# Queries and keys of the first block: their halves exchanged by DMA inside SBUF instead of by a product with a permutation matrix

## The reference, cut to what matters

```python
proj = h @ w_in[l]
q, k, v, iq, ik, iw, z, xbc, dt_raw, ga, gm = jnp.split(proj, SPLIT_POINTS, axis=-1)
q = apply_rope(rms_norm(q.reshape(bsz, seq, 16, 64), q_norm_g[l]), cos, sin)
k = apply_rope(rms_norm(k.reshape(bsz, seq, 16, 64), k_norm_g[l]), cos, sin)
...
iq = apply_rope(iq.reshape(bsz, seq, 8, 64), cos, sin)
ik = apply_rope(ik[:, :, None, :], cos, sin)[:, :, 0, :]

def apply_rope(x, cos, sin):
    x1, x2 = jnp.split(x, 2, axis=-1)
    return jnp.concatenate([x1 * c - x2 * s, x2 * c + x1 * s], axis=-1)
```

## Time and profile before

| | us |
|---|---|
| median of three runs (lowest, highest) | 2292.93 (2292.71, 2293.42) |
| the profiled execution's own time | 2292.45 |
| its span, first to last instruction | 2290.4 |
| PE busy in the span | 2165.0 (95%) |
| DVE, ACT, POOL busy | 1653.6 (72%), 1425.2 (62%), 201.7 (9%) |
| DMA | 395.25 MB, mean 173 GB/s |

### The profile page before, as it was taken

How to read it: one execution, slowest core, us unless ns; L and a number is a source line. 1 busy time by engine, 2 the same in 40 slices (tenths; PEclk the granted TensorE clock), 3 DMA queues, 4 the chain that set the end, 5 groups by cost and what they waited for, 6 DMA issues and landing times.

```text
span 2290.4 us, 42346 instructions
## 1 busy us (share of the span) xinstructions
PE 2165.0 (95%) x17416; PEld 2068.5 (90%) x17416; DVE 1653.6 (72%) x2994; ACT 1425.2 (62%) x2226; POOL 201.7 (9%) x178
## 2 busy tenths in 40 slices
PE   2989999999999899999999998899999998899999
PEld 2979889999999798999999997799999997899999
DVE  5898778578769987686779873556788673557654
ACT  2678897366545788874665655864654557764542
POOL 0000000022100000000223110100030111000000
PEclk9999999999999999999999998999999999999999
DMA  7545556567755554565565531345565423345664
GB/s 281 199 161 180 175 175 227 188 201 237 232 191 192 174 167 157 203 229 182 169 188 167 171 106 54 126 147 185 186 192 176 148 86 103 120 155 165 193 187 127
DMA packets 110592, 395.25 MB, mean 173 GB/s; under 512 B 12320, under 2 KB 13888, under 8 KB 110272
## 3 DMA queue, kind: packets, MB, share of 16 engines
q1 hardware_dynamic: 96768, 344.09, 46.1%
q0 software_dynamic: 11904, 43.03, 5.7%
q10 hardware_dynamic: 1728, 5.43, 0.6%
HBM read 391.46 MB, written 1.05 MB: 171 GB/s over the span
## 4 chain that ended last, share of the span: by engine, by line
PE 73%; DVE 12%; ACT 11%; issue 2%; DMA 1%; SPq 0%; ACTq 0%; DVEq 0%
PE bank L553 72%; ACT scr L1086 4%; DVE WL L1638 3%; ACT WH L1086 3%; ACT L1075 2%; ACT arena L1086 2%; DVE arena L1734 2%; DMA ring<-in_w 1%; DVE arena L2396 1%; DVE scr L1930 1%; PE bank L637 1%; DVE scr L1717 1%; DVE scr L1917 1%; DVE small L1929 0%; DVE scr L2003 0%
## 5 line engine op out<-in xcount | busy, mean ns | idle before, releaser
L1086 ACT ACTIVATE WH<-ring 128x1024 fp32r<-128x1024 f32 (+1 forms) x638 | 669.4, 1052 | 684.1 <-PE bank L553 665.4
L553 PE MATMUL bank<-HTH,WH 128*128 128x256 f32 (+1 forms) x3408 | 977.8, 287 | 13.5 <-DVE HTL L1707 4.7
L553 PE MATMUL bank<-HTL,WH 128*128 128x256 f32 (+1 forms) x3408 | 962.0, 282 | 0.0
L553 PE MATMUL bank<-HTH,WL 128*128 128x256 f32 (+1 forms) x3408 | 961.3, 282 | 0.0
L1638 DVE TENSOR_TENSOR WL<-ring,WH 128x1024 fp32r<-128x1024 f32 (+2 forms) x602 | 729.1, 1219 | 169.2 <-ACT WH L1086 166.7
L553 PEld LDWEIGHTS bank<-HTH,WH 128*128 128x128 f32 (+1 forms) x3408 | 646.1, 190 | 25.8 <-issue 6.9
L553 PEld LDWEIGHTS bank<-HTL,WH 128*128 128x128 f32 (+1 forms) x3408 | 646.0, 190 | 3.1 <-issue 2.6
L553 PEld LDWEIGHTS bank<-HTH,WL 128*128 128x128 f32 (+1 forms) x3408 | 645.8, 190 | 0.1
L1075 ACT ACT_TABLE_LOAD x123 | 157.8, 1283 | 33.9 <-PE bank L553 16.4
L553 PE MATMUL bank<-ff2h,WH 128*128 128x256 f32 x512 | 143.8, 281 | 0.0
L553 PE MATMUL bank<-ff2l,WH 128*128 128x256 f32 x512 | 143.8, 281 | 0.0
(11 more groups left out here) (332 smaller groups left out, 3624.1 us busy)
## 6 DMA issues: line engine op xcount, KB each, us to landing
ring<-in_w SPq DMA_DIRECT2D x620, 512.0 KB, 4.1
arena<-in_wada POOLq DMA_DIRECT2D x80, 512.0 KB, 4.8
ring<-in_w SPq DMA_DIRECT2D x24, 384.0 KB, 3.3
arena<-in_wada SPq DMA_DIRECT2D x8, 512.0 KB, 19.0
arena<-in_wada ACTq DMA_DIRECT2D x8, 512.0 KB, 21.7
XT<-in_xt SPq DMA_DIRECT2D x1, 1024.0 KB, 9.0
arena<-in_s POOLq DMA_DIRECT2D x4, 256.0 KB, 3.7
ring<-in_w SPq DMA_DIRECT2D x8, 128.0 KB, 2.0
```

The lines of the kernel that those rows point to most:

```text
L553: ins = e.matmul(out, a, b, start=(start and i == 0), stop=(stop and i == len(pairs) - 1))
L1086: return e.activation(out, a, func, **kw)
```

## The change

The product with `perm` leaves the rope blocks on PE: `rope_pe` goes, step 11 keeps the sums over a head, step 12 is empty on PE. POOL instead waits for DVE's "gain" at the unit of step 11 (and 22) and issues four DMAs, each of 32 partitions by 1024 floats, that write q and k of the block with the halves exchanged into the lane's two scratch tiles; DVE waits for the last of them (`swapped`) and multiplies in place by the sine. As the exchange has no sign, the sine's table is multiplied once at the start by a column of -1 and 1 on ACT, and `perm` (still used for `iq` and `ik`) has only ones. In `A_TICKS` the rotation, step 12 and step 23, falls three units after the gain instead of two, and the steps behind it move one unit later.

```diff
-                put["perm"][m + 32, m] = -1
+                put["perm"][m + 32, m] = 1
...
+    put["sgn"][:] = np.where(p % 64 < 32, -1, 1)
...
-    "attn0": [5, 7, 9, 11, 13, 15, 17, 19, 21, 23, 25, 27, 29, 31, 33, 35, 39, 41, 43, 45, 47, 51, 53, 55, 57, 59, 61,
-              63, 65, 67, 69, 71],
-    "attn1": [5, 7, 9, 11, 13, 15, 18, 20, 22, 24, 31, 33, 35, 37, 39, 41, 43, 45, 47, 49, 51, 55, 57, 59, 61, 63, 65,
-              67, 69, 71, 73, 75],
+    "attn0": [5, 7, 9, 11, 13, 15, 17, 19, 21, 23, 25, 27, 30, 32, 34, 36, 39, 41, 43, 45, 47, 51, 53, 56, 58, 60, 62,
+              64, 66, 68, 70, 72],
+    "attn1": [5, 7, 9, 11, 13, 15, 18, 20, 22, 24, 31, 33, 36, 38, 40, 42, 44, 46, 48, 50, 52, 55, 57, 60, 62, 64, 66,
+              68, 70, 72, 74, 76],
...
+        QK = ar(0, 2, 2048)
...
     (tensor engine)
-                p.wait_ge(L.V("gain", l, bi))
-                mm(L.b[0][0:n, :], [(perm, xq)])
-                mm(L.b[1][0:n, :], [(perm, xk)]).then_inc(L.P.inc("turn", l, bi), 1)
-                yield
...
     (scalar engine, at the start)
-            act(trig[:, 1, :], x, ACT.Sin).then_inc(start_scalar.inc(), 1)
+            act(trig[:, 1, :], x, ACT.Sin).then_inc(start_scalar.inc("sine"), 1)
+            p.wait_ge(in_cst("in"), start_scalar("sine"))
+            act(trig[:, 1, :], trig[:, 1, :], ACT.Identity, scale=con("sgn")).then_inc(start_scalar.inc(), 1)
...
     (vector engine)
-                p.wait_ge(L.P("turn", m, bi), L.V("gain", m, bi))
+                p.wait_ge(swapped[L is LB](m, bi), L.V("gain", m, bi))
-                    e.tensor_tensor(v2(s[i]), v2(b[i]), twice(sinap), ALU.mult).then_inc(L.V.inc(), 1)
+                    e.tensor_tensor(v2(s[i]), v2(s[i]), twice(sinap), ALU.mult).then_inc(L.V.inc(), 1)
...
     (GpSimd, after the issue of the ada tile of the same u)
+                    for par in range(2):
+                        L, tile = (LA, LB)[par], scr[:, 2 * par:2 * par + 2, :]
+                        for bi, slot in ((par, 11), (par + 2, 22)):
+                            if u - plan.base[2 * l] == A_TICKS["attn%d" % par][slot]:
+                                p.wait_ge(L.V("gain", l, bi))
+                                for b in range(4):
+                                    to, of = slice(32 * b, 32 * b + 32), slice(32 * (b ^ 1), 32 * (b ^ 1) + 32)
+                                    e.dma_start(tile[to], QK[of, :, 512 * bi:512 * bi + 512]).then_inc(
+                                        swapped[par].inc(*((l, bi) if b == 3 else ()), by=16), 16)
```

More of the change, by code:

```diff
@@ L41 @@
 CONSTS = [("id", 128), ("ones", 128), ("blk", 128), ("perm", 128), ("dup", 64), ("tri0", 256),
-          ("mask", 256), ("rot", 256), ("scan", 256), ("invf", 1), ("eps", 1), ("same", 32)]
+          ("mask", 256), ("rot", 256), ("scan", 256), ("invf", 1), ("eps", 1), ("sgn", 1), ("same", 32)]
 def const_columns():
@@ L362, in program @@
         cst = sb("cst", [128, NCON])
-        cols = sb("cols", [128, NCOL + 30])
+        cols = sb("cols", [128, NCOL + 29])
         rows = sb("rows", [128, 128])
@@ L476, in program @@
         opened = sig("opened")
+        swapped = [sig("swapped_a"), sig("swapped_b")]
         FREED_BY_VECTOR = {"su", "xc", "ao", "so", "res", "up", "pe", "b0", "b1", "b2"}
@@ L600, in attn @@
                 for bi in (par, par + 2):
-                    yield from rope_pe(L, l, bi, flat(Q[:, 2 * bi:2 * bi + 2, :]), flat(K[:, 2 * bi:2 * bi + 2, :]),
-                                       con("blk"), con("perm"), 128)
+                    yield
+                    p.wait_ge(L.A("sq", l, bi))
+                    mm(L.b[0][:, :], [(con("blk"), L.s[0])])
+                    mm(L.b[1][:, :], [(con("blk"), L.s[1])]).then_inc(L.P.inc("ss", l, bi), 1)
+                    yield
+                    yield
                     for pr in (2 * bi, 2 * bi + 1):
@@ L608, in attn @@
                                            lambda h, t: VV[:, t, 64 * h:64 * h + 64], ev_scalar("v", l, 3, 2 * l))
-            def rope_pe(L, l, bi, xq, xk, ones, perm, n):
-                yield
[L613 to L616, removed]
-                p.wait_ge(L.V("gain", l, bi))
-                mm(L.b[0][0:n, :], [(perm, xq)])
-                mm(L.b[1][0:n, :], [(perm, xk)]).then_inc(L.P.inc("turn", l, bi), 1)
-                yield
             def pair_pe(L, l, pr, before, bi, q, k, v, v_ready):
@@ L1845, in rope_dve @@
             def rope_dve(L, m, bi, xq, xk, gq, gk, cosap, sinap, n):
-                s, b = [t[0:n, :] for t in L.s], [t[0:n, :] for t in L.b]
+                s = L.s
                 yield
```

## The result

The changed kernel takes **2303.97 us** (median of four runs, 2301.12 to 2304.64) where the kernel before takes 2292.82 (four runs): ratio 1.0046, interval 1.0028 to 1.0063. It is 11 us slower; the prediction had 2289.3, and a chance of 0.12 for slower. The profiled execution took 2301.12 us (span 2299.0).

What follows compares the result with a forecast made beforehand. PE held 73% of the chain, with DVE or ACT setting the pace in stretches; 0.1 + 1.3 + 0.4 is 1.8 us a layer, 3.6 in both, from 2292.45 to 2288.8 profiled, median 2289.3; 8-in-10 range 2281 to 2296.

Steps and rivals of the forecast that it cites:

- DVE's and ACT's other work only moves by a unit: Last sentence on added costs: the remaining DVE and ACT steps just shift by one unit, at no cost.
- 0.4 gained: First mixer behind B2, chain on ACT: fewer table loads save up to 0.8 us of a PE wait; 0.4 taken.
- The clock: Rival: the new 3.2 us PE wait at B2 halves the clock, costing 3.4 us in both layers, 2292.7; chance 0.13.
- A1 and B1: First two rope blocks of each mixer: DVE and ACT lead from gain to k, so together 0.1 us is kept.
- y at A1: PE's y product of `ssd` at A1: without the product covering it, PE waits for L2003 until 159.7.
- B1's k: Rotated k at B1: ready at 196.0, PE there at 195.1, so PE waits 0.9 us.
- A1's k: Rotated k at A1: ready at 170.9, PE there at 171.0; no new wait, but none to spare.
- the late-tile rival: Ada tile behind the exchanges takes 7.5 us, not 4.8; PE waits for k, 3.2 us slower, 2296.1; chance 0.17.
- A2 and B2: Last two rope blocks of each mixer: A2 keeps 1.8 us, B2 waits 3.2; together 1.2 to 1.3 kept.
- The DMAs: 32 exchanges of 128 KB on POOL: landing about 6 us after the gain; cost nothing, at worst 0.6 at A1.
- PE's time is kept whole: Rival: all the product's PE time in the mixers is saved, 14.6 us, giving 2278.3; chance 0.13.

Runs made afterwards that it cites:

- e1: The kernel before with only the new `A_TICKS`, the product with `perm` staying on PE: 2306.29 us, ratio 1.0063.
- f2: The kernel after with every step behind a rotation one unit later, except the first of them, which stays: 2294.34 us, ratio 1.0001.
- g4: The kernel after with six useless 256-column products on PE before its wait for k at B2: 2300.23 us, ratio 1.0037.
- e4: The kernel after with the exchange of halves left out altogether (no product, no DMA), new `A_TICKS`: 2298.66 us, ratio 1.0030.
- f1: The kernel after with every step behind a rotation one unit later, at odd units: 2288.12 us, ratio 0.9980.
- f3: The kernel before, exchange by the product with `perm`, with the same odd-unit steps as f1: 2302.30 us, ratio 1.0042.
- e3: The kernel after with the exchange of halves left out altogether (no product, no DMA) and the old `A_TICKS`: 2292.78 us, ratio 0.9997.
- e2: The kernel after, exchange by DMA, with the old `A_TICKS`: 2296.50 us, ratio 1.0016.

## Why the prediction was wrong

**The step that failed** is the last sentence of what is added: "DVE's and ACT's other work only moves by a unit", costed at nothing. I had counted table loads, and had them right (119, four fewer than 123), but not in what order they fall. Against my sum, counted at unit starts: from unit 38 to 52 the kernel after loses 1.6 us a mixer, and from 64 to 76 another 1.5, where I had 0.4 gained. That is 3.5 a mixer, 7.0 in all. Of the 3.1 lost, 0.75 is the transposes' wait behind an `Exp` at an even unit at unit 50, and 1.0 is what the wait at unit 70 (1.58) has more than the one that stood in that stretch before (0.54). Some 0.9 more is seven further interruptions of PE's units, estimated as above, which my sum didn't have either. e1 has the same 1.6 and 1.5 without any DMA; in f2 they are 0.65 and, in the first mixer, 0.9.

**The clock** (rival, 0.13) came true at B2 in both mixers: 3.4 us by its price, some 3.0 by what g4 gets back. I had priced it nearly right and held it to be unlikely; but my own forecast contained the idling of 3.2 us that brings it. It belonged in the sum.

**A1 and B1.** y at A1: forecast 159.7, measured 159.69. B1's k: wait of 0.9 forecast, 0.65 measured in the first mixer and 1.59 in the second. A1's k had none to spare and was late by 0.8 in both. The ada tile, issued at 160.76 as forecast, took 5.6 us and not 4.8, and at B1 of the second mixer 7.5: the late-tile rival, in part. From 0.1 kept it became 0.5 lost in the first mixer and 1.5 in the second: 2.2 in both. e4, without an exchange, keeps 0.3 a mixer there, so this is the DMAs' cost, which the prediction had at nothing.

**A2 and B2.** A2: 1.7 of 1.8 kept. B2: wait of 3.2 forecast, 2.9 measured. Over both, 1.3 kept was forecast; without the clock's 1.7 it is 0.9 and 0.8. So right in place, and 0.9 short in both mixers.

**The DMAs.** Issued 0.54 apart, each landing some 2.8 us after its issue (median; 4.4 at most), and DVE never waits for them ahead of a rotation: as forecast. That they cost nothing was wrong: the kernel after and e4, the same without them, are 2.2 us apart in the profiled executions (2301.12, 2298.95), which is what A1 and B1 show. One working in the prediction is off and changes nothing: with the last issue at 1.9 and its estimate of 2.3 to land, the exchange is there 4.2 after the gain, not 4.5.

The forecast for the profiled execution, 2288.8, with these terms put right, is 2288.8 + 7.0 + 3.4 + 2.2 + 0.9 = 2302.3. Less the net 1.3 us that this execution gains behind unit 76, which no mechanism here explains, it is 2301.0; it took 2301.12. So the sum closes that well by a term that isn't understood. The rival "PE's time is kept whole" is what f1 against f3 shows for this exchange at equal units, 14.2 us. It isn't to be had in this order of work, since the units that free k cost 9.3 of it.

## What to carry to other kernels

In an order written out by hand, the cost of moving a step isn't its own time: it is what it now stands behind on its engine (here an evacuation and two table loads), what it no longer stands in front of (here y's wait), and whether it opens one more interruption of the main work (here some 0.13 us each). List them for every moved step, before counting any saving. And where PE is given less to do, ask how long it now idles at one stretch: a wait near 3 us was mostly followed by half the clock, and the run in which the product was simply deleted was no faster.

## What the runs showed of the hardware that I had not expected

- Six useless matmuls of 256 columns in a wait of 2.9 us kept the granted clock at 1.00 in both mixers, where it was 0.50 without them.
- With PE work deleted (e3) the median of a run's mean granted clock was 0.984, where the kernel before had 0.988; 0.004 go with some 2 to 7 us of 2290.
- Four transfers of 128 KB within SBUF, queued ahead of a 512 KB tile from HBM, delay it by their issue (2.2 us), and it then took 5.6 and 7.5 us in two cases where the median of its kind is 4.8. The earlier trace rows has a tile of 7.5 us with no exchange ahead of it, so the exchanges are not shown to be the cause of that.
- A transfer of 128 KB within SBUF mostly lands 2.8 us after its issue, but one took 6.44 (e2).
